# Four dense feed forwards: two compensated products of the rounded fp32 type in place of three of bf16

## The chip, the cores and the metric

The kernel runs on one core of one Trainium2 chip. The metric is the device time of one execution in microseconds. TensorE (PE in the rows), VectorE (DVE), ScalarE (ACT), GpSimd (POOL) and the DMA queues are driven by programs of their own, which wait for each other by semaphores. SyncE (SP) issues the transfers of the weights.

## The reference, cut to what matters

The model is a stack of four layers over 256 tokens of 1024 channels; the first layer also carries 256 context tokens. Each layer has a mixer and a feed forward. The feed forwards touched here are dense and gated:

```python
def swiglu(t, w_gate, w_up, w_down):
    return (silu(t @ w_gate) * (t @ w_up)) @ w_down
x = x + g2 * swiglu(modulate(x, n_ffn, sh2, sc2), wg, wu, wd)
```

All inputs are fp32. There are four such calls: the first layer's on x (hidden width 2816), the same weights on the context (2816), the second layer's (2816) and the third layer's (3584). The fourth layer has eight experts in its place, of which each token uses two; they are computed by other code (`moe_parts`), which stays as it is.

## The kernel before, in words

**Tiling.** A feed forward goes over the hidden width in chunks of 128: 22, 22, 22 and 28 chunks, 94 in all. A chunk's weights are 1.5 MB: the front (gate and up, 128 partitions x 2048 fp32 values, 1 MB) and the back (down, 128 x 1024, 0.5 MB). They come into a ring of four slots in SBUF (`RING`), by the SP queue (`feed`, L334), which issues front c+1 and then back c, each after a wait until the slot's old front or back is released (`front_used`, `back_used`). The plan of the ring goes over the whole program: two blocks of modulation weights stand ahead of each feed forward, one or three behind some of them (`early`, `behind` in the new text; `ada_n`, `behind` in the old).

**Products.** To get near fp32 from bf16, each operand is split in a bf16 head and a bf16 remainder, and each product is made of three: head x head, head x remainder, remainder x head. For a chunk, `up_products` (L971) does the first layer: for gate and up, and for 8 blocks of 128 channels, three products (L984 to L986) with the weights stationary and the 256 tokens moving, so 48 with 256 columns. `down_products` (L989) does the second layer: two token blocks x two halves of the 1024 outputs x three products (L999 to L1001), 12 with 512 columns, the hidden tokens stationary. The outputs stay in four PSUM banks over all chunks.

**Splits.** ScalarE casts the front and the back to bf16 (`cast_hi_loop`, L1190 and L1193; `cast_hi`, L954 and L957, outside the loop). VectorE subtracts (`make_lo`, L964 and L968) and so makes the remainder, writes it to a buffer of its own, and releases the slot at that moment. Heads and remainders have two buffers each, by the chunk's parity. The input of the feed forward is split the same way once (L1091, L1122).

**Order.** PE does first layer c+1, then second layer c, and so on. ScalarE for chunk c: silu (`silu_of`, L1009), cast of front c+2, cast of back c+1. VectorE for chunk c (`gate_of`): product of the silu and the up part (L1016), its cast to bf16 (L1024), its remainder (L1026), then the remainders of front c+2 (L964) and back c+1 (L968). The chunks run in a hardware loop of four per round, with the last two or more outside. At the start of a feed forward the first front is cast and split in halves (L1094, L1095, L1126, L1129), between modulation rows (L494, L502). At its end VectorE multiplies the four banks by the gate row and adds them to x (L1173, L1176), and ScalarE squares (L540).

**The rounded type.** The projections of the mixers (`split_linear`, L767) already split fp32 operands in two parts of the rounded four-byte type (named fp32r where it is written, f32 where products read it) and do three products of it (L830 to L832), with 288 to 512 columns. Their remainders are written over the raw weights in the ring (L875).

The expert code has a second form for many tokens to an expert (`ffn_parts` with `gates`), which is not executed on these inputs; the change keeps it under the name `general_parts`.

Of the kernel before, what the change touches and what calls it, by code (L numbers as in the profile page):

```python
# [19 lines left out]
F32 = mybir.dt.float32  # L20
# [43 lines left out]
FFNS = ("l0_ffn", "l1_ffn", "ffn2", "moe")  # L64

# [42 lines left out]
class Signals:  # L108


    def __init__(self, sig):
# [46 lines left out]
        self.block_made = sig("last_group_block")  # L158

# [57 lines left out]
def build(nc, ctx, d, out):  # L217
# [33 lines left out]
    RINGR = halves_of("weights", SLOTS * SLOT)  # L251
    PS = ctx.enter_context(nc.psum_tensor("ps", [PB, 8, 512], F32))
# [718 lines left out]
    def up_products(pe, j, n, hid, width, h_hi, h_lo, by_half=False):  # L971

        if by_half:
            pe.wait_ge(S.w_lo.sem, S.w_lo.at(1))
        else:
            pe.wait_ge(front_used.sem, n + (place.n + 1))
        pe.wait_ge(S.act_done.sem, n + S.act_done.at(1))
        for w in range(2):
            if by_half and w:
                pe.wait_ge(front_used.sem, place.n + 1)  # L980
# [55 lines left out]
    def ffn_parts(x, f, o, gates=None, gate=GB, first=0, ada_at=None, ada_n=0, behind=0):  # L1036

        a, n = place.n, f // PB * (NE if gates is not None else 1)  # L1040
# [3 lines left out]
        h = HT[:, :, o:o + T]  # L1044
# [4 lines left out]
        def products(pe):  # L1049
# [4 lines left out]
            for i in range(ada_n):  # L1054
                ada_row(pe, i, ada_at)
            zero_products(pe, 2 if ada_n else 14, 5)
            pe.wait_ge(S.h_lo.sem, S.h_lo.at(2))

            def up(j, n, by_half=False):
                up_products(pe, j, n, hid, T, lambda k: h_hi[:, k, :], lambda k: h_lo[:, k, :], by_half)  # L1060
            up(0, 0, gates is None)
            for i in range(ada_n):
                ada_turn(pe, i)
# [8 lines left out]
            for i in range(min(2, behind)):  # L1072
                ada_row(pe, i, a + n, ada_n)
            for i in range(behind):
                ada_turn(pe, i, ada_n)
                if i + 2 < behind:
                    ada_row(pe, i + 2, a + n, ada_n)
            zero_products(pe, max(0, 18 - 8 * behind), 4)

        def squares(act):  # L1080
            for i in range(4):
                if i < behind:
                    ada_row_kept(act, i, ada_n)
                act.wait_ge(S.tail_added.sem, S.tail_added.at(i + 1))
                part_square(act, first + i // 2, i % 2, x[:, i // 2, i % 2 * 512:(i % 2 + 1) * 512])
                if 0 < i <= behind:
                    ada_cols_kept(act, i - 1, a + n, ada_n)

        def silus(act):
            for half in halves:  # L1090
                act.activation(h_hi[:, half, :], h[:, half, :], ACT.Copy).then_inc(S.h_hi.sem, 1)  # L1091
            if gates is None:
                act.wait_ge(front_in[place.n % SLOTS].sem, 16 * (place.n // SLOTS + 1))
                act.activation(gu[0][0][:, 0:D], RING[:, place.n % SLOTS, 0:D], ACT.Copy).then_inc(S.w_hi.sem, 1)  # L1094
                act.activation(gu[0][0][:, D:2 * D], RING[:, place.n % SLOTS, D:2 * D],  # L1095
                               ACT.Copy).then_inc(S.hi_gu.sem, 1)
            for i in range(ada_n):
                ada_row_kept(act, i)
            if gates is None:
                cast_hi(act, 0, 1, 1)  # L1100
                cast_hi(act, 1, 0, 0)
            for i in range(ada_n):
                ada_cols_kept(act, i, ada_at)
# [11 lines left out]
            squares(act)  # L1115

        def gating(dve):
# [6 lines left out]
            if gates is None:  # L1124
# [6 lines left out]
                dve.wait_ge(S.ada_kept.sem, S.ada_kept.at(ada_n))  # L1131
                dve.sem_inc(front_used.sem, 1)
                make_lo(dve, 0, 1, 1)
                make_lo(dve, 1, 0, 0)
            if ada_n:
                ada_bias(dve, ada_n, ada_at)
            if gates is None:
# [1540 lines left out]
```

## Time and profile before

| what | value |
|---|---|
| median of 3 runs | 2676.68 us (2670.01 to 2681.77) |
| span of the profiled execution | 2666.8 us |
| time of that execution beside its span | not given; the median stands 9.9 us above the span |
| busy share of the span: PE / DVE / ACT | 92% / 70% / 55% |
| mean granted TensorE clock | 0.973 |
| HBM read | 671.79 MB, 252 GB/s over the span |

The execution begins with the first layer's mixer; the dense feed forwards of the first layer run from 306 to 665 us, the second layer's from about 1005, the third layer's from about 1365; the experts fill the time from 1770 us on. A product's recorded duration holds its way through the array and overlaps with the next, so the distance from one start to the next tells what a product costs.

### The profile page before, as it was taken

To read this page: it belongs to the slowest core of one execution; us is meant where nothing else is said; L and a number is where in the kernel's file an instruction comes from. 1 tells how busy PE (TensorE), PEld (TensorE's weight loads), DVE (VectorE), ACT (ScalarE), POOL (GpSimd) and SP (SyncE) were. 2 spreads that over 40 slices of the span, in tenths; PEclk is the share of its full clock that TensorE was granted. 3 is DMA by queue.
4 is the path that set the end of the run, shared out by engine and by line. 5 is a ranking of instruction groups with operands and counts; after the bars stand their busy time and mean duration, and the time that the engine had idled before them with its cause. 6 is when DMAs were issued, how large, how long until landed. Compare 5 with 4: busy or idle time off the path is not lost. (4 is left out here: it accounts for less than half of the span.)

```text
span 2666.8 us, 58450 instructions
## 1 busy us (share of the span) xinstructions
PE 2458.1 (92%) x23209; PEld 1851.2 (69%) x23209; DVE 1880.0 (70%) x2489; ACT 1466.4 (55%) x1865; POOL 14.9 (1%) x12
## 2 busy tenths in 40 slices
PE   6988999999898889999899999889999899999997
PEld 4745777677664457768677768667777777777775
DVE  3277555655645566555765555769999999999997
ACT  3146444433421545434454434458888888888885
POOL 0000000000200000000000000000000000000000
PEclk9989999999988999999999999999999999999999
DMA  7340555554456126555375545439999999999995
GB/s 302 116 200 25 223 199 208 214 199 163 150 223 243 75 89 259 207 186 183 140 276 192 210 174 185 163 113 396 411 417 414 417 418 407 419 416 418 418 417 232
DMA packets 121213, 674.38 MB, mean 253 GB/s; under 512 B 13489, under 2 KB 13969, under 8 KB 67089
## 3 DMA queue, kind: packets, MB, share of 16 engines
q1 hardware_dynamic: 120032, 664.47, 64.1%
q10 hardware_dynamic: 1072, 8.42, 0.8%
q8 instruction: 74, 1.21, 0.2%
q14 instruction: 35, 0.28, 0.0%
HBM read 671.79 MB, written 1.05 MB: 252 GB/s over the span
## 5 line engine op out<-in xcount | busy, mean ns | idle before, releaser
L984 PE MATMUL ps<-projected,normed_or_mix 128*128 128x256 bf16 x1504 | 409.9, 273 | 1.5 <-issue 1.5
L985 PE MATMUL ps<-projected,normed_or_mix 128*128 128x256 bf16 x1504 | 409.9, 273 | 0.0
L1383 DVE TENSOR_TENSOR aux<-weights,aux 128x1024 bf16<-128x1024 f32 x223 | 271.2, 1217 | 1.4 <-ACT aux L1329 1.4
L1378 DVE TENSOR_TENSOR turned<-weights,turned 128x2048 bf16<-128x2048 f32 x112 | 256.3, 2288 | 8.9 <-ACT turned L1323 4.2
L1323 ACT ACTIVATE turned<-weights 128x2048 bf16<-128x2048 f32 x112 | 213.6, 1907 | 49.7 <-DMA weights<-moe 47.3
L1329 ACT ACTIVATE aux<-weights 128x1024 bf16<-128x1024 f32 x223 | 232.1, 1041 | 2.1 <-PE ps L1267 1.8
L1254 PE MATMUL ps<-projected,turned 128*128 (+1 forms) x1792 | 232.9, 206 | 0.0
L1253 PE MATMUL ps<-projected,turned 128*128 (+1 forms) x1792 | 232.9, 206 | 0.0
L1255 PE MATMUL ps<-projected,turned 128*128 (+1 forms) x1792 | 232.9, 206 | 0.0
L831 PE MATMUL ps<-weights_halves,normed_or_mix_halves 128*128 128x512 f32 (+4 forms) x576 | 218.6, 380 | 0.0
L1265 PE MATMUL ps<-aux,probs 128*96 128x512 bf16 x448 | 172.6, 385 | 43.4 <-DVE probs L1393 43.4
L986 PE MATMUL ps<-projected,aux 128*128 128x256 bf16 x752 | 205.0, 273 | 0.0
L986 PE MATMUL ps<-projected,normed_or_mix 128*128 128x256 bf16 x752 | 205.0, 273 | 0.0
L1016 DVE TENSOR_TENSOR probs_turned<-probs,ps 128x256 f32<-128x256 f32 x94 | 39.5, 421 | 229.3 <-ACT probs L1009 229.3
L1009 ACT ACTIVATE probs<-ps 128x256 f32<-128x256 f32 x94 | 36.0, 383 | 295.4 <-PE ps L986 295.1
L1254 PEld LDWEIGHTS ps<-projected,turned 128*128 128x128 bf16 x1792 | 175.4, 98 | 6.5
L1253 PEld LDWEIGHTS ps<-projected,turned 128*128 128x128 bf16 x1792 | 175.3, 98 | 5.1
L1255 PEld LDWEIGHTS ps<-projected,turned 128*128 128x128 bf16 x1792 | 175.3, 98 | 0.0
L875 DVE TENSOR_TENSOR weights_halves<-weights,extra_halves 128x948 fp32r<-128x948 f32 (+4 forms) x80 | 92.7, 1165 | 111.9 <-ACT extra_halves L856 111.9
L1267 PE MATMUL ps<-aux,probs 128*96 128x512 bf16 x448 | 169.8, 379 | 0.0
L1266 PE MATMUL ps<-aux,probs 128*96 128x512 bf16 x448 | 169.8, 379 | 0.0
L984 PEld LDWEIGHTS ps<-projected,normed_or_mix 128*128 128x128 bf16 x1504 | 147.5, 98 | 29.4 <-issue 3.4
(399 smaller groups left out, 6365.8 us busy)
## 6 DMA issues: line engine op xcount, KB each, us to landing
weights<-moe SPq DMA_DIRECT2D x224, 1024.0 KB, 8.5
weights<-moe SPq DMA_DIRECT2D x224, 512.0 KB, 6.6
weights<-l_ffn SPq DMA_DIRECT2D x66, 1024.0 KB, 4.9
weights<-ada SPq DMA_DIRECT2D x64, 1024.0 KB, 5.6
weights<-l_ffn SPq DMA_DIRECT2D x66, 512.0 KB, 5.6
weights<-ada SPq DMA_DIRECT2D x64, 512.0 KB, 6.0
weights<-ffn SPq DMA_DIRECT2D x28, 1024.0 KB, 4.9
weights<-w_in SPq DMA_DIRECT2D x24, 948.0 KB, 4.8
```

The costliest lines, as they stand in the source:

```text
L831: pe.matmul(o, h_hi(k)[:, t], lo, start=False, stop=False)
L984: pe.matmul(o, hi, h_hi(k), start=(k == 0), stop=False)
L985: pe.matmul(o, hi, h_lo(k), start=False, stop=False)
L986: mm = pe.matmul(o, lo, h_hi(k), start=False, stop=(k == KD - 1))
L1253: pe.matmul(o, hi[:, t], xh, start=(k == 0), stop=False)
L1254: pe.matmul(o, hi[:, t], xl, start=False, stop=False)
L1255: mm = pe.matmul(o, lo[:, t], xh, start=False, stop=(k == KD - 1))
L1265: pe.matmul(o, hi, w_hi[:, t], start=start, stop=False)
L1323: act.activation(gu4[j % SLOTS][0], RING[:, slot(j), 0:2 * D], ACT.Copy).then_inc(S.hi_gu.sem, 1)
L1329: act.activation(down4[j % SLOTS][0], RING[:, slot(j), 2 * D:3 * D], ACT.Copy).then_inc(S.hi_d.sem, 1)
L1378: dve.tensor_tensor(gu4[j % SLOTS][1], RING[:, slot(j), 0:2 * D], gu4[j % SLOTS][0], ALU.subtract).then_inc(front_used.sem, 1)
L1383: dve.tensor_tensor(down4[j % SLOTS][1], RING[:, slot(j), 2 * D:3 * D], down4[j % SLOTS][0], ALU.subtract).then_inc(back_used.sem, 1)
```

## The change: what it does

In the four dense feed forwards each operand a is split as a lead and a rest of the rounded four-byte type, with L = 128. For a weight w: lead = w / (L + 1), rest = w - L x lead. For an input or hidden value h: lead = L x h, rest = (L + 1) x h - lead. Then w x h is (lead of w) x (lead of h) + (rest of w) x (rest of h) up to what the rounding leaves in second order: two products in place of three.

- `ffn` is written out for itself; the three closures of `ffn_parts` remain for the experts' second form only.
- PE: 2 x 8 x 2 = 32 products for a chunk's first layer, 8 for its second. The rests of the weights are read from the ring itself.
- ScalarE: scaled copies make the leads of the weights, and now also the lead of the hidden product, after the copy of front c+2.
- VectorE: one multiply-add with an immediate makes each rest, and writes a weight's rest over its slot. The rest of the hidden product stands behind the rest of front c+2.
- PE, not VectorE, releases the slots: the front at the end of a first layer, the back at the end of a second.
- The first chunk is still split in halves, and the modulation rows keep their place.

```diff
+LEAD = 128.0
+        h_lead, h_rest = (PR[:, i * 2048:(i + 1) * 2048].rearrange("p (k t) -> p k t", k=KD) for i in range(2))
+        w_lead = [[XNR[:, 0:2 * D], XNR[:, 2 * D:3 * D]], [AUXR[:, 0:2 * D], XNR[:, 3 * D:4 * D]]]
+        f_lead = [PbR[:, p * 512 + T:p * 512 + 2 * T] for p in range(2)]
+        f_rest = [PTR[:, p * 512 + T:p * 512 + 2 * T] for p in range(2)]
...
+        def lead_of(act, to, src):
+            return act.activation(to, src, ACT.Copy, scale=1 / (LEAD + 1))
+
+        def rest_of(dve, to, src, lead):
+            return dve.scalar_tensor_tensor(out=to, in0=lead.bitcast(F32), scalar=-LEAD, in1=src, op0=ALU.mult,
+                                            op1=ALU.add)
+
+        def up(pe, j, c, first=False):
+            if first:
+                pe.wait_ge(S.w_lo.sem, S.w_lo.at(1))
+            else:
+                pe.wait_ge(S.rest_gu.sem, c + S.rest_gu.at(1))
+            pe.wait_ge(S.prod.sem, c + S.prod.at(1))
+            for w in range(2):
+                if first and w:
+                    pe.wait_ge(S.rest_gu.sem, S.rest_gu.at(1))
+                    pe.wait_ge(S.ada_kept.sem, S.ada_kept.at(early))
+                for k in range(KD):
+                    t = w * D + k * PB
+                    out_ = hid[j % 2][:, w * T:(w + 1) * T]
+                    pe.matmul(out_, w_lead[j % 2][0][:, t:t + PB], h_lead[:, k, :], start=(k == 0), stop=False)
+                    mm = pe.matmul(out_, ring(RINGR, j, t, t + PB), h_rest[:, k, :], start=False, stop=(k == KD - 1))
+            mm.then_inc(front_used.sem, 1)
+
+        def down(pe, j, c, last=False):
+            pe.wait_ge(S.rest_d.sem, c + S.rest_d.at(1))
+            pe.wait_ge(S.hid_rest.sem, c + S.hid_rest.at(1))
+            for b in range(2):
+                for hf in range(2):
+                    q, t = slice(b * PB, (b + 1) * PB), hf * 512
+                    pe.matmul(PS[:, 2 * b + hf, :], f_lead[j % 2][:, q], w_lead[j % 2][1][:, t:t + 512], start=False,
+                              stop=False)
+                    mm = pe.matmul(PS[:, 2 * b + hf, :], f_rest[j % 2][:, q],
+                                   ring(RINGR, j, PART + t, PART + t + 512), start=False, stop=last)
...
+            mm.then_inc(back_used.sem, 1)
...
+        def silu_and_lead(act, j, c, gate_up=lambda: None):
+            p = j % 2
+            act.wait_ge(front_used.sem, c + (c0 + 1))
+            act.wait_ge(S.prod.sem, c + S.prod.at(1))
+            act.activation(silu[p], hid[p][:, 0:T], ACT.Silu).then_inc(S.silu_done.sem, 1)
+            gate_up()
+            act.wait_ge(S.prod.sem, c + S.prod.at(3))
+            act.wait_ge(back_used.sem, c + (c0 - 1))
+            act.activation(f_lead[p], f_of[p], ACT.Copy, scale=LEAD).then_inc(S.hid_lead.sem, 1)
...
+        def product_and_rest(dve, j, c, gate_up=lambda: None):
+            p = j % 2
+            dve.wait_ge(S.silu_done.sem, c + S.silu_done.at(1))
+            dve.tensor_tensor(f_of[p], silu[p], hid[p][:, T:2 * T], ALU.mult).then_inc(S.prod.sem, 1)
+            gate_up()
+            dve.wait_ge(S.hid_lead.sem, c + S.hid_lead.at(1))
+            dve.scalar_tensor_tensor(out=f_rest[p], in0=f_of[p], scalar=LEAD + 1, in1=f_lead[p].bitcast(F32),
+                                     op0=ALU.mult, op1=ALU.subtract).then_inc(S.hid_rest.sem, 1)
...
+                with pe.Fori(0, rounds) as g:
+                    for j in range(SLOTS):
+                        up(pe, j + 1, g * SLOTS + (j + 1))
+                        down(pe, j, g * SLOTS + j)
...
+                with act.Fori(0, rounds) as g:
+                    for j in range(SLOTS):
+                        c = g * SLOTS
+                        silu_and_lead(act, j, c + j, lambda: gate_up_lead(act, j + 2, c + (j + 2), g))
+                        down_lead(act, j + 1, c + (j + 1), g)
...
+                with dve.Fori(0, rounds) as g:
+                    for j in range(SLOTS):
+                        c = g * SLOTS
+                        product_and_rest(dve, j, c + j, lambda: gate_up_rest(dve, j + 2, c + (j + 2)))
+                        down_rest(dve, j + 1, c + (j + 1))
```

## Rows read from the trace of the kernel before

**Rows 1.** The page, busy tenths of PE, and GB/s, in 40 slices.
```profile
PE   6988999999898889999899999889999899999997
GB/s 302 116 200 25 223 199 208 214 199 163 150 223 243 75 89 259 207 186 183 140 276 192 210 174 185 163 113 396 411 417 414 417 418 407 419 416 418 418 417 232
```

**Rows 2.** Windows: stretch, its us, busy us of each engine, clock, DMA share, GB/s.
```profile
340.00:475.00 135.00, 135.00 (x1036) 101.21 (x1035) 77.63 (x85) 59.37 (x56) 0.00 (x0) 1.00 0.56 201
```

**Rows 3.** Groups of instructions by line (busy us, mean ns of one, idle before).
```profile
L984 PE MATMUL ps<-projected,normed_or_mix 128*128 128x256 bf16 x1504 | 409.9, 273 | 1.5 <-issue 1.5
L1009 ACT ACT_TABLE_LOAD x16 | 20.5, 1283 | 54.6 <-PE ps L986 54.4
```

**Rows 4.** Timeline of one chunk: start us, duration us, instruction [idle before].
```profile
340.65 0.27 PE L984 MATMUL ps<-projected,normed_or_mix 128*128 128x256 bf16 x1
340.65 0.10 PEld L985 LDWEIGHTS ps<-projected,normed_or_mix 128*128 128x128 bf16 x1
...
345.89 0.38 PE L999 MATMUL ps<-aux,probs 128*128 128x512 bf16 x1
...
348.48 0.27 PE L984 MATMUL ps<-projected,normed_or_mix 128*128 128x256 bf16 x1
```

**Rows 5.** Timeline of the projection's last two groups, 512 and 288 columns.
```profile
754.69 0.39 PE L830 MATMUL ps<-extra_halves,normed_or_mix_halves 128*128 128x512 f32 x1
...
758.09 0.29 PE L830 MATMUL ps<-extra_halves,normed_or_mix_halves 128*128 128x288 f32 x1
758.09 0.19 PEld L831 LDWEIGHTS ps<-weights_halves,normed_or_mix_halves 128*128 128x128 f32 x1
758.22 0.19 PEld L832 LDWEIGHTS ps<-extra_halves,turned_halves 128*128 128x128 f32 x1
...
762.06 0.29 PE L830 MATMUL ps<-extra_halves,normed_or_mix_halves 128*128 128x288 f32 x1
```

**Rows 6.** Timeline of ScalarE and VectorE around a table load.
```profile
340.47 2.29 DVE L964 TENSOR_TENSOR aux<-weights,normed_or_mix 128x2048 bf16<-128x2048 f32 x1 [0.59 <-ACT normed_or_mix L1190]
342.68 1.22 DVE L968 TENSOR_TENSOR normed_or_mix<-weights,normed_or_mix 128x1024 bf16<-128x1024 f32 x1
...
346.15 1.28 ACT L1009 ACT_TABLE_LOAD   x1 [4.18 <-PE ps L986]
347.44 0.38 ACT L1009 ACTIVATE probs<-ps 128x256 f32<-128x256 f32 x1
347.72 1.90 ACT L1190 ACTIVATE normed_or_mix<-weights 128x2048 bf16<-128x2048 f32 x1
...
349.66 2.29 DVE L964 TENSOR_TENSOR normed_or_mix<-weights,normed_or_mix 128x2048 bf16<-128x2048 f32 x1 [0.59 <-ACT normed_or_mix L1190]
```

**Rows 7.** Lines by themselves (ns min/median/max) and groups of multiply-adds (busy us, mean ns).
```profile
L856 ACT ACTIVATE projected_halves<-weights x32: 1042/1057/1128, 244.5 to 1745.0; 128x1024 fp32r<-128x1024 f32 x32
L1193 ACT ACTIVATE aux<-weights x42: 1045/1057/1059, 321.0 to 1549.1; 128x1024 bf16<-128x1024 f32 x42
L2517 DVE SCALAR_TENSOR_TENSOR normed_or_mix<-x_sb,small,row_params 128x1024 f32<-128x1024 f32 x2 | 2.5, 1283 | 0.0
L2065 DVE SCALAR_TENSOR_TENSOR aux<-aux 128x512 f32<-128x512 f32 x2 | 1.4, 684 | 0.0
```

**Rows 8.** DMA issues of the page: KB each, median us from issue to landing.
```profile
weights<-l_ffn SPq DMA_DIRECT2D x66, 1024.0 KB, 4.9
```

**Rows 9.** Timeline at the first feed forward's start and end.
```profile
312.46 2.29 DVE L964 TENSOR_TENSOR aux<-weights,normed_or_mix 128x2048 bf16<-128x2048 f32 x1 [0.76 <-ACT normed_or_mix L954]
...
315.90 1.40 PE L502 MATMUL ps<-square_consts,k_turned 128*128 128x3 f32 x12
...
322.40 0.38 PE L999 MATMUL ps<-normed_or_mix,probs 128*128 128x512 bf16 x1
...
482.44 0.69 DVE L1173 TENSOR_TENSOR extra<-ps,gate_rows 128x512 f32<-128x512 f32 x1 [1.61 <-PE ps L1001]
...
489.11 2.00 ACT L1091 ACTIVATE projected<-turned 128x1024 bf16<-128x1024 f32 x2 [0.46 <-PEq L1200]
```

More of the change, by code:

```diff
@@ L1034, in ffn_done, with general_parts @@
             s.done(n)
-    def ffn_parts(x, f, o, gates=None, gate=GB, first=0, ada_at=None, ada_n=0, behind=0):
-        a, n = place.n, f // PB * (NE if gates is not None else 1)
+    def general_parts(x, f, gates, gate=GB):
+        a, n = place.n, f // PB * NE
         hid = [PS[:, 4 + p, :] for p in range(2)]
@@ L1071, in products @@
                 down_products(pe, c, c, outs, stop=(c == n - 1), each=S.bank_done if c == n - 1 else None)
[L1072 to L1087, printed above, removed]
+            zero_products(pe, 18, 4)
         def silus(act):
@@ L1195, in ffn @@
     def ffn(x, f, o, gate=GB, first=0, behind=0):
-        a, n, beside = place.n, f // PB, 2
-        place.n += beside
-        products, silus, gating = ffn_parts(x, f, o, gate=gate, first=first, ada_at=a, ada_n=beside, behind=behind)
+        a, n, early = place.n, f // PB, 2
+        c0 = a + early
+        hid = [PS[:, 4 + p, :] for p in range(2)]
+        h = HT[:, :, o:o + T]
+        h_lead, h_rest = (PR[:, i * 2048:(i + 1) * 2048].rearrange("p (k t) -> p k t", k=KD) for i in range(2))
@@ L1202, in _ @@
             def _(sp):
-                feed(sp, a + SLOTS, a + beside + n + behind + SLOTS)
+                feed(sp, a + SLOTS, c0 + n + behind + SLOTS)
             @block.tensor
             def _(pe):
-                products(pe)
+                for bank in range(4):
+                    pe.matmul(PS[:, bank, :], Z16[:, 0:PB], Z16[:, :], start=True, stop=False)
+                for i in range(early):
+                    ada_row(pe, i, a)
+                zero_products(pe, 2, 5)
+                pe.wait_ge(S.h_lo.sem, S.h_lo.at(2))
@@ L1213, in _ @@
+                for i in range(4):
+                    if i < behind:
+                        ada_row_kept(act, i, early)
+                    act.wait_ge(S.tail_added.sem, S.tail_added.at(i + 1))
+                    part_square(act, first + i // 2, i % 2, x[:, i // 2, i % 2 * 512:(i % 2 + 1) * 512])
+                    if 0 < i <= behind:
+                        ada_cols_kept(act, i - 1, c0 + n, early)
             @block.vector
             def _(dve):
[L1215 to L1216 removed]
```

206 lines of the change are left out of this document (124 added, 82 removed).

## The prediction

> **What bounds the kernel now.** I read the page first [rows 1]: TensorE is busy in nine tenths or more of most slices until the experts begin, and there the transfers take over, at over 400 GB/s. The change touches only the four dense feed forwards, so the next view is the windows [rows 2]: inside a feed forward PE is busy all the time (135.00 of 135.00 us), VectorE 58% of it, ScalarE 44%, the DMA engines 56%, at a granted clock of 1.00, which is the 2.4 GHz level. So the feed forwards are bound by TensorE and by nothing else. The groups [rows 3] give the counts: L984 has 1504 products, so 94 chunks of 16, and three products for each pair.
>
> The durations in those groups (273 ns) overlap, so I take the time from one start to the next from the timeline [rows 4]. The first layer's products of one chunk run from 340.65 to 345.89: 48 in 5.24 us, 0.109 each. The second layer's run from 345.89 to 348.48: 12 in 2.59 us, 0.216 each. Together 7.83 us, and 94 x 7.83 = 736 us, 28% of the span.
>
> **The change, part by part.**
>
> *First layer's products.* 48 of bf16 with 256 columns become 32 of the rounded type with 256. No row shows that type at 256 columns. The nearest rows are the projections [rows 5]: at 512 columns 15 steps take 3.40 us (0.2267 each), at 288 columns 30 steps take 3.97 us (0.1323 each). Between them a column costs 0.42 ns, and 32 columns below the narrower one give 0.119. The bounds: 0.109, the bf16 pitch at the same width, since four-byte operands showed no gain anywhere; and 0.132, the 288 pitch, which holds whatever part of it is a floor under narrow products. I take 0.119, as it is nearest to the 288 row. So 32 x 0.119 = 3.80 us, 1.44 less. The weight load is the point of doubt: recorded at 0.19 us for four bytes, 0.10 for bf16 [rows 4, 5]. But at 288 columns the next load starts 0.13 us after the last one, while the last one is still on record, so loads overlap each other and the products.
> A rule speaks against this. The Trainium skill, TensorE: Matmul & The Clock Gate, section "The mechanism" (what overlaps and what doesn't), lets a load overlap running products only when it targets another row group; its section "LDWEIGHTS (loading the stationary operand)" gives 128/1.2 = 107 ns. By these an estimate is 32 x (107 + 107) ns + 8 x (107 + 213) ns = 9.4 us a chunk. The trace disagrees for both types: a bf16 load of 0.10 and a product of 107 ns fit in a pitch of 0.109.
>
> *Second layer's products.* 12 become 8 at 512 columns: 8 x 0.2267 = 1.81 us, 0.78 less. A chunk on PE is then 5.61 us, 2.22 less.
>
> *ScalarE.* The two casts become scaled copies into the four-byte type, and the cast of the hidden product moves here from VectorE. The type costs nothing: 1057 ns in L856 and in L1193 for 1024 columns [rows 7]. Busy per chunk: 1.90 + 1.06 + 0.38 (silu) + 0.38 (new; same size as the silu) = 3.7 us, below 5.61.
>
> *VectorE.* Subtractions become a multiply-add with an immediate, written over the slot. Such an operation costs what a subtraction costs (L2065, 512 columns, 684 ns, against 0.69 for one of two tensors), and with two pointers and 1024 columns 1283 ns against 1.22 us [rows 6, 7, 9]. I take 2.29 + 1.22 + 0.42 + 0.43 = 4.4 us; 0.13 more if the pointer form is right. Under 5.61 again. The cast L1024 goes.
>
> *The new chain.* A chunk's second layer needs its hidden remainder, and on VectorE that now stands behind the remainder of the gate and up weights two chunks ahead, which waits for ScalarE. From the moment PE leaves the first layer [rows 4, 6]: 0.26 until ScalarE starts, 0.28 to its next instruction, 1.94 for the lead cast and the handover (347.72 to 349.66), 2.21 to the next VectorE instruction (340.47 to 342.68), 0.43, and 0.06 to PE: 5.18 us. PE has 1.81 + 3.80 = 5.61 us of other products, so this is hidden by 0.4. A table load adds 1.29 (346.15 to 347.44): 6.47, a stall of 0.86. There are 16 [rows 3]: one at the start of each of three feed forwards, and 13 in the loops, one in each later round of four. 13 x 0.86 = 11 us is given back.
> The Trainium skill, ScalarE: Activation LUTs, section "What ACT_TABLE_LOAD costs", adds a drain of 1.38 us to each load. With it the sum would lose 18 us more, an estimate. The silu at 347.44 stands right behind the load, so the trace shows no drain.
>
> *Slots.* A slot's front is now released by PE at the end of its products, not by VectorE, and the SP queue issues in the order front, back, so each issue waits for PE. Front c+4 is issued when the first layer of c ends and is needed by ScalarE two chunks later, 11.2 us on; it lands in 4.9 us (median) [rows 8]. Traffic rises from 201 GB/s to 1.57 MB per 5.61 us = 280 GB/s, against 417 reached in the experts [rows 1, 2]. At the ends, the last slots are freed by PE within its last 9 us instead of before them; but the block behind starts at 489.1, 6.7 us after the first of VectorE's final additions, and first asks for modulation rows, whose slots are freed earlier [rows 9]. I cost all this at nothing; its cover is those margins.
>
> *Start.* [rows 9] In the first feed forward VectorE finishes the second chunk's front at 314.75, unchanged. PE's first chunk now ends near 314.4, the turns of the modulation rows (1.4 us) follow, and the second chunk's first layer ends at 319.6. But the first second layer waits for the chain: table load near 316.1, silu 317.4, lead 317.65 to 319.55, remainder to 321.8, hidden remainder 322.2. Before, it began at 322.40. So the two first chunks' first layers gain nothing, 0.1 us in all; where no table load stands at the start (the context's feed forward) 1.3 more.
>
> *End.* VectorE's eight final operations from 482.44 on, 0.69 each, set the end, started by the first bank; of the last second layer only one bank's share (0.2) is gained, and about 0.15 lost to the hidden chain (1.96 us against 1.81).
>
> **Sum.** With 22 chunks: 20 x 1.44 + 21 x 0.78 + 0.15 = 45.3 us, three times, plus 1.3: 137. With 28: 26 x 1.44 + 27 x 0.78 + 0.15 = 58.6. Together 196, less 11 for the table loads: 185 us. The profile gives no time of its execution beside the span of 2666.8; 2666.8 - 185 = 2481.8, and the median of the runs stands 9.9 above the span, so **2492 us**.
> Bounds by the pitch: at 0.109 (and 0.216) the same sum is 230 - 16 = 213, 2464 us. At 0.132 it is 159 - 6 = 153, 2524 us.
>
> **The rivals.**
> 1. *Each load shows (slower).* If at 256 columns a four-byte load isn't hidden, a first layer's product costs 0.188 + 0.107 = 0.295: 9.4 + 1.8 = 11.2 us a chunk, 3.4 more, 94 times: 2998 us. By the page's rule above, with 9.4 us a chunk, it would be about 2825, an estimate. The point that decides is (7.83 - 1.81) / 32 = 0.188 a product, 42% above the 288 row. For it: the doubled load record and that no row is as narrow. Against it: rows 5. 3%.
> 2. *VectorE paces (no change).* If the multiply-add into the four-byte type took two passes, its 2048 and 1024 columns would take 4.4 and 2.3 us, the hidden one 0.7: 7.8 us a chunk, what it is now, near 2675 us. For it: no row has it that long. Against: 1283 ns at 1024. 3%.
> 3. *The transfers pace.* If holding the slots longer kept the rate at the present 205 GB/s or little above, a chunk would take 1.57 MB / 0.22 TB/s = 7.1 us and save 0.7: 94 x 0.7 = 66 us, 2611. For it: every issue now waits for PE. Against: two chunks of slack. 5%.
> 4. *The chain shows in every chunk.* If handovers add 0.7 us to 5.18, it exceeds 5.61 by 0.27; a held second layer delays the next but one first layer, so half of that shows in each chunk: 94 x 0.14 = 13 us, and 13 x 0.7 = 9 at the table loads: 2514. It has only 0.4 us of cover. 9%, inside the range.
>
> The forecast with its bounds has 80%. **Range** 2462 to 2535: from the lower bound to beyond the upper one, with rival 4 in it; rivals 1 to 3 are left out. About 0.5% (13 us) is what a measurement of this kernel can tell from no change. Faster by more: 0.8 + 0.05 + 0.09 = 0.94; within it 0.03; slower 0.03.
>
> **What would show it.** In the changed profile: 40 products a chunk, 32 of them starting 0.119 apart and 8 at 0.227; table loads 22.4 + 0.9 = 23.3 us apart; after each load a gap on PE of 0.9 us before the second layer, and none elsewhere; VectorE's 2048-column rows at 2.29; ScalarE waiting for PE, never for a landing; granted clock 1.00; the experts unchanged at about 417 GB/s. I am wrong if the pitch at 256 columns is over 0.132, if PE idles before a first layer (released by VectorE's remainder: rival 2; with ScalarE waiting for DMA: rival 3), or if the second layer waits in every chunk (rival 4).

## The result, and the profile after

| | before | after |
|---|---|---|
| median, four runs of each | 2675.76 us (2670.01 to 2681.77) | 2511.55 us (2505.05 to 2511.93) |
| span of the profiled execution | 2666.8 us | 2503.3 us |
| its own time | not given | 2505.05 us |

The ratio of the medians is 0.9381 (0.9361 to 0.9401): faster. The forecast was 2492 us with a range of 2462 to 2535, so it was 20 us too low and the range holds the result.

The page of the changed kernel, 40 slices of the span: busy tenths of PE, granted clock, GB/s (they answer to [rows 1]).

```profile
PE   6988999998977789999999899889999999999997
...
PEclk9979999999988999999999998999999999999999
...
GB/s 306 134 218 1 127 269 255 276 278 198 148 228 267 1 165 258 267 193 182 193 271 269 273 174 133 138 346 417 411 417 415 418 418 408 418 417 418 417 417 214
```

The experts are as they were, at 417 GB/s. In the middle of the feed forwards the transfers rose from about 200 to between 255 and 278 GB/s. The same shows in the windows (stretch, its us, busy us of PE, PEld, DVE, ACT and POOL, granted clock, DMA share, GB/s); the two short ones are the first second layers of the first and the third of the four feed forwards (the first layer's and the second layer's):

```profile
340.00:475.00 135.00, 128.66 (x898) 115.30 (x899) 95.27 (x96) 84.08 (x103) 0.00 (x0) 1.00 0.74 268
326.50:329.70 3.20, 3.12 (x8) 2.49 (x9) 3.20 (x3) 1.01 (x2) 0.00 (x0) 0.51 0.62 246
944.00:948.00 4.00, 3.54 (x10) 2.90 (x11) 4.00 (x5) 1.39 (x2) 0.00 (x0) 0.57 0.57 226
```

In [rows 2] PE was busy for 135.00 of 135.00 us; now 6.3 us of that stretch are not. VectorE went from 58% to 71%, ScalarE from 44% to 62%. PE is still what the chunks go by, but something holds it up now and then. The timeline of PE over one chunk (start us, duration us, instruction):

```profile
341.28 0.28 PE L1180 MATMUL ps<-projected_halves,normed_or_mix_halves 128*128 128x256 f32 x1
341.39 0.28 PE L1181 MATMUL ps<-projected_halves,weights_halves 128*128 128x256 f32 x1
...
345.11 0.40 PE L1190 MATMUL ps<-normed_or_mix_halves,probs_halves 128*128 128x512 f32 x1
...
346.95 0.28 PE L1180 MATMUL ps<-projected_halves,aux_halves 128*128 128x256 f32 x1
```

Read against [rows 4]: 32 products in 3.83 us, 0.1197 each, then 8 in 1.84 us, 0.230 each. A chunk is 5.67 us where it was 7.83. What holds PE up is on the timeline of all engines around a table load (in brackets the idle time before an instruction and what ended it), the counterpart of [rows 6]:

```profile
345.37 1.28 ACT L1216 ACT_TABLE_LOAD   x1 [2.30 <-PE ps L1181]
346.67 0.38 ACT L1216 ACTIVATE probs<-ps 128x256 f32<-128x256 f32 x1
346.95 1.90 ACT L1161 ACTIVATE normed_or_mix_halves<-weights 128x2048 fp32r<-128x2048 f32 x1
348.75 0.41 ACT L1220 ACTIVATE probs_halves<-probs_turned 128x256 fp32r<-128x256 f32 x1
...
348.88 2.29 DVE L1164 SCALAR_TENSOR_TENSOR weights_halves<-normed_or_mix_halves,weights 128x2048 fp32r<-128x2048 f32 x1 [1.38 <-ACT normed_or_mix_halves L1161]
351.10 0.42 DVE L1237 SCALAR_TENSOR_TENSOR probs_turned_halves<-probs_turned,probs_halves 128x256 fp32r<-128x256 f32 x1
351.66 0.47 PE L1190 MATMUL ps<-normed_or_mix_halves,probs_halves 128*128 128x512 f32 x1 [0.71 <-DVE probs_turned_halves L1237]
...
369.02 1.28 ACT L1216 ACT_TABLE_LOAD   x1 [2.30 <-PE ps L1181]
```

PE leaves the first layer at 345.11. The load, the silu, the lead of the gate and up weights two chunks ahead, its rest, and then the rest of the hidden product stand in line, and PE gets that last one 6.55 us later. The next load stands 23.65 us behind this one; four chunks are 4 x 5.67 = 22.68, so each load costs 0.97 us: 0.88 before the second layer (6.55 - 5.67), and about 0.08 more because its first product after a wait takes 0.30 us to the next one, not 0.23.

At the start of the first feed forward the same chain shows at its full length, and the products behind it are slow:

```profile
320.29 1.28 ACT L1216 ACT_TABLE_LOAD   x1
...
321.86 1.91 ACT L1161 ACTIVATE normed_or_mix_halves<-weights 128x2048 fp32r<-128x2048 f32 x1
...
326.01 0.42 DVE L1237 SCALAR_TENSOR_TENSOR probs_turned_halves<-probs_turned,probs_halves 128x256 fp32r<-128x256 f32 x1
326.58 0.77 PE L1190 MATMUL ps<-normed_or_mix_halves,probs_halves 128*128 128x512 f32 x1 [2.64 <-DVE probs_turned_halves L1237]
327.14 0.63 PE L1192 MATMUL ps<-weights_halves,probs_turned_halves 128*128 128x512 f32 x1
...
329.92 0.28 PE L1180 MATMUL ps<-projected_halves,normed_or_mix_halves 128*128 128x256 f32 x1
```

PE idles 2.64 us, and then its second-layer products start 0.43 us apart instead of 0.23: the granted clock in that window is 0.51, the lower of its two levels (1.2 GHz). This second layer takes 3.34 us instead of 1.84; of the difference 1.4 us are the clock's, since one that begins after a wait at the full clock takes 1.92 (the third layer's in this profile). The waits by what they were for (us in total, times, longest) say who is late and who isn't:

```profile
ACT probs L1216 <- PE ps L1181: 156.6, 74, 2.7
...
DVE weights_halves L1164 <- ACT normed_or_mix_halves L1161: 66.3, 49, 1.5
...
DVE weights_halves L1164 <- ACT aux_halves L1161: 42.9, 43, 1.4
...
ACT L1216 <- PE ps L1181: 29.9, 13, 2.3
```

ScalarE waits for PE, VectorE for ScalarE; in no row does ScalarE wait for a transfer inside the feed forwards.

**Where the time went, by stage.** From the timeline I took each feed forward from ScalarE's first copy of its input to the end of the mean-square chain behind it, and what lies between them, in us of one profile each:

| | FF 1 | context | FF 2 | FF 3 | the four | span less the four |
|---|---|---|---|---|---|---|
| before | 183.13 | 185.59 | 187.81 | 234.78 | 791.31 | 1875.5 |
| after | 144.86 | 140.20 | 148.93 | 182.51 | 616.50 | 1886.8 |

The four feed forwards, which are all that the change touches, gave 174.8 us. The rest, whose code is the same, took 11.3 us more in this profile: 4.1 in the stretch from 136 us to the first feed forward, 1.8 between the context's and the second layer's, 0.4 between the second and the third layer's, 5.1 in the mixer behind the third layer's, nothing in the experts. The next section looks at whether that is the change's.

### The profile page after: what moved, and what is told of

Same layout as the page of the kernel before. It is cut to its first block and busy times, and to the rows that moved or that the text cites. A ratio compares the mean times of both kernels' runs of the same rounds, so it can differ in the third digit from the quotient of the medians.

```text
span 2503.3 us, 54795 instructions
## 1 busy us (share of the span) xinstructions
PE 2268.8 (91%) x21306; PEld 1811.3 (72%) x21329; DVE 1844.2 (74%) x2395; ACT 1490.5 (60%) x1959; POOL 14.9 (1%) x12
## 3 DMA queue, kind: packets, MB, share of 16 engines
HBM read 671.79 MB, written 1.05 MB: 269 GB/s over the span
## 5 line engine op out<-in xcount | busy, mean ns | idle before, releaser
L1181 PE MATMUL ps<-projected_halves,weights_halves 128*128 128x256 f32 x1504 | 364.9, 284 | 0.0
L1181 PEld LDWEIGHTS ps<-projected_halves,weights_halves 128*128 128x128 f32 x1504 | 288.6, 192 | 3.4
L1164 DVE SCALAR_TENSOR_TENSOR weights_halves<-normed_or_mix_halves,weights 128x1024 fp32r<-128x1024 f32 (+1 forms) x145 | 222.6, 1537 | 66.3 <-ACT normed_or_mix_halves L1161 66.3
L1161 ACT ACTIVATE normed_or_mix_halves<-weights 128x1024 fp32r<-128x1024 f32 (+1 forms) x145 | 188.8, 1304 | 10.9 <-PE ps L1192 10.9
L1180 PE MATMUL ps<-projected_halves,normed_or_mix_halves 128*128 128x256 f32 x752 | 182.5, 284 | 1.5 <-issue 1.5
L1180 PE MATMUL ps<-projected_halves,aux_halves 128*128 128x256 f32 x752 | 182.5, 284 | 0.0
L1190 PE MATMUL ps<-normed_or_mix_halves,probs_halves 128*128 128x512 f32 x376 | 151.0, 402 | 18.9 <-DVE probs_turned_halves L1237 18.5
```

The source lines that it names most:

```text
L1161: return act.activation(to, src, ACT.Copy, scale=1 / (LEAD + 1))
L1164: return dve.scalar_tensor_tensor(out=to, in0=lead.bitcast(F32), scalar=-LEAD, in1=src, op0=ALU.mult, op1=ALU.add)
L1180: pe.matmul(out_, w_lead[j % 2][0][:, t:t + PB], h_lead[:, k, :], start=(k == 0), stop=False)
L1181: mm = pe.matmul(out_, ring(RINGR, j, t, t + PB), h_rest[:, k, :], start=False, stop=(k == KD - 1))
```

## Experiments

### The two kernels again

Edit: none in either.

> The kernel before once more, nothing edited, to see what its stages repeat. Theory (the stages that the change doesn't touch move by some us with the granted clock, in either kernel): the stretch from the first rotary step to the first feed forward and the one of the last scan mixer differ by 2 to 6 us from the first profile, the four feed forwards stay at 183.1, 185.6, 187.8 and 234.8 within 1 us. Rival (the stages repeat to a tenth of a us, and the changed kernel's 11 us more are its own): every stretch as in the first profile.

> The changed kernel once more, nothing edited, to see what repeats. Theory (all that the change does lies in the four feed forwards, the rest of the difference is the TensorE clock in stages it doesn't touch): the four feed forwards take 144.9, 140.2, 148.9 and 182.5 us again within 2 us each, a round of four chunks 23.65 us, while the stages before the first feed forward and between them move by some us either way, with the granted clock. Rival (the change lengthens the other stages by 11 us, by its place in the program or by what it leaves behind): those stages show the same +4.0, +1.8, +0.5 and +5.1 us as in the first profile. Ratio to before 0.938 in both.

**Measured.** The kernel before: 2673.4 us in one run, the feed forwards 183.13, 185.59, 187.80 and 234.78, the same to 0.01 us. The changed kernel: 2507.23 us against 2679.3 beside it, ratio 0.9361 (0.9332 to 0.9389); its feed forwards took 144.97, 140.19, 148.91 and 183.93, in sum 618.00. The third layer's is 1.4 us longer than in the first profile, and in this one the granted clock fell at its start too.

**What follows.** The feed forwards repeat, so an effect can be read from their sum to within 1.5 us, which is what one fall of the clock makes. The rest doesn't: in the two profiles of the kernel before, the stretch from 136 us to the first feed forward is 170.1 and 172.5 us long, the last mixer 164.7 and 168.9. In the changed one they are 174.3 and 170.4, and 169.8 and 164.7, and there the granted clock goes with it: from 136 to 180 us it was 0.57 in the longer and 0.77 in the shorter. The experts move too: 901.9 and 902.0 us before, 901.8 in the first profile of the changed kernel and 910.4 in the second, with nothing edited between these two. So single stages of the same code differ by 2 to 9 us from profile to profile.

Whether the sum of these stages is longer for the changed kernel is less clear. The span less the feed forwards is 1875.5 and 1880.3 us for the kernel before, and 1886.8 and 1887.2 for the changed one. For the two-product kernel below, whose code is the old one but for the products left out, it is 1886.8 as well, so the new code is not needed for it. The median less the feed forwards is:

| runs beside each other | before | changed kernel and its variants |
|---|---|---|
| the first (four each) | 1884.5 | 1895.1 |
| changed kernel again and the next three below | 1888.0 | 1889.2, 1890.1, 1890.0, 1888.6 |
| narrower products, PE busy (one run each) | 1881.6, 1882.1 | 1893.1, 1893.3 |
| both starts mended | 1890.0 | 1891.3 |

Twice it is 1 to 2 us more, and twice about 11. So the 11 us are not shown to be the change's, nor shown not to be: that stays open.

### One silu ahead of the loop

```diff
                 down_lead(act, 0, 0)
+                act.activation(SM[:, 250:251], SM[:, 250:251], ACT.Silu)
                 for i in range(early):
```

> ScalarE does one silu of one column ahead of the modulation copies, before the loop of each feed forward, so that the table is already loaded when the loop begins. Theory (the 13 loads inside the loops each hold the second layer by 0.96 us, and the three at the start sit in the chain to the first second layer): table loads in the feed forwards fall from 16 to 3, one before each of the three loops, a round takes 22.7 us instead of 23.65, the idle of PE before the first second layer falls from 2.6 to 1.3 us as in the context's feed forward, and the time falls by 13 x 0.96 + 3 x 1.3 + 3 for the clock behind the idle, about 19 us: ratio to before 0.931. Rival (the loads are hidden and the gap has another cause, the remainders on VectorE): rounds stay at 23.65 and the time within 3 us of the changed kernel. Second rival: the load is placed in the loop again, 16 remain, nothing changes.

**Measured.** 2487.72 us, ratio 0.9296 (0.9270 to 0.9323); the feed forwards 597.62 us, 20.4 less than the changed kernel run beside it. The table loads of L1216 are gone from all rounds, and three are left, at the new line (the line by itself, and the timeline at the start of the first feed forward, with PE's first second layer in it and in the second and third layers'):

```profile
L1283 ACT ACT_TABLE_LOAD  x3: 1283/1283/1283, 315.9 to 1242.6; - x3
```

```profile
315.92 1.28 ACT L1283 ACT_TABLE_LOAD   x1
317.22 0.20 ACT L1283 ACTIVATE small<-small 128x1 f32<-128x1 f32 x1
...
318.80 0.39 ACT L1216 ACTIVATE probs<-ps 128x256 f32<-128x256 f32 x1
...
323.98 0.47 PE L1190 MATMUL ps<-normed_or_mix_halves,probs_halves 128*128 128x512 f32 x1 [1.55 <-DVE probs_turned_halves L1237]
...
935.65 0.47 PE L1190 MATMUL ps<-normed_or_mix_halves,probs_halves 128*128 128x512 f32 x1 [1.35 <-DVE probs_turned_halves L1237]
...
1250.41 0.47 PE L1190 MATMUL ps<-normed_or_mix_halves,probs_halves 128*128 128x512 f32 x1 [1.35 <-DVE probs_turned_halves L1237]
```

**What follows.** This is a one-column instruction that computes nothing that is used. It makes the silu's table the one that stands when the loop is entered, and then the program loads none inside. In the changed kernel, as in the one before, a load stood in every round of three feed forwards, though silus and plain copies are all that ScalarE does there. The load now lies in idle time of ScalarE. The sum fits: 13 stalls of 0.97 are 12.6 us; in three starts the wait falls from 2.6 us to 1.55, 1.35 and 1.35, together 3.6; and the clock stays up after the shorter wait, three times 1.4 us: 20.4.

### The hidden product's split ahead of the weights'

```diff
             act.activation(silu[p], hid[p][:, 0:T], ACT.Silu).then_inc(S.silu_done.sem, 1)
-            gate_up()
...
             act.activation(f_lead[p], f_of[p], ACT.Copy, scale=LEAD).then_inc(S.hid_lead.sem, 1)
+            gate_up()
```

The same on VectorE: the rest of the hidden product stands ahead of the rest of the gate and up weights.

> The hidden product's lead and rest go ahead of the next front's lead and rest, on ScalarE and on VectorE. Theory (the order in the change hides the handover between the two engines; with the hidden values first, each turn of VectorE holds product 0.45, ScalarE's lead of the hidden 0.30, its copy of the front 1.94, the front's rest 2.21 and the back's rest 1.15, 6.05 us in a ring, over PE's 5.67): a chunk takes 6.05 us, table loads no longer show at PE, about 0.38 x 90 - 13 = 21 us more than the changed kernel, ratio to before 0.946. Rival (the chain to the second layer is what costs, and shortening it pays): no gap behind table loads, a round at 22.7 us, 12 us less than the changed kernel, ratio 0.934.

**Measured.** 2518.05 us, ratio 0.9403 (0.9374 to 0.9432); the feed forwards 628.09 us, 10.1 more than the changed kernel. A wait at the first layer takes the place of the one at the second (timeline of ScalarE and PE):

```profile
346.28 0.40 PE L1190 MATMUL ps<-normed_or_mix_halves,probs_halves 128*128 128x512 f32 x1
...
348.46 0.39 PE L1180 MATMUL ps<-projected_halves,normed_or_mix_halves 128*128 128x256 f32 x1 [0.18 <-DVE weights_halves L1164]
...
349.90 0.42 ACT L1219 ACTIVATE probs_halves<-probs_turned 128x256 fp32r<-128x256 f32 x1 [2.61 <-DVE probs_turned L1234]
...
352.38 0.40 PE L1190 MATMUL ps<-normed_or_mix_halves,probs_halves 128*128 128x512 f32 x1
...
358.44 0.40 PE L1190 MATMUL ps<-normed_or_mix_halves,probs_halves 128*128 128x512 f32 x1
```

A chunk is 358.44 - 352.38 = 6.06 us, where 5.67 of PE's are products.

**What follows.** In this order the two engines make a ring: lead of the weights on ScalarE, rest of the weights and of the back on VectorE, the next hidden product behind them, its lead on ScalarE, and only then the next lead of weights. Its length of 6.06 us is in every chunk, so the order that the change chose is the better one in the steady state; the chain that it leaves has 0.4 us of room except at a table load. The ring's length was foreseen to 0.01 us, the effect on the time only by half (21 expected, 10.1 measured in the feed forwards). The expectation left out the starts: the waits before the four first second layers (9.2 us in the second profile of the changed kernel) and the slow clock behind three of them (4.3) are gone here, and in three starts a wait of 1.4 us before the third chunk's first layer takes their place. That makes about 11.6 of the 21; the rest isn't told apart.

### Two bf16 products in place of three

The kernel before with two of its three products in the dense feed forwards; its casts, its remainders and its order stay. It leaves out a product that near-fp32 results need, so it only serves to tell the count of the products from their type.

```diff
                 pe.matmul(o, hi, h_hi(k), start=(k == 0), stop=False)
-                pe.matmul(o, hi, h_lo(k), start=False, stop=False)
                 mm = pe.matmul(o, lo, h_hi(k), start=False, stop=(k == KD - 1))
...
                 pe.matmul(PS[:, bank, :], hi[:, o], w_hi[:, c], start=start, stop=False)
-                pe.matmul(PS[:, bank, :], hi[:, o], w_lo[:, c], start=False, stop=False)
-                mm = pe.matmul(PS[:, bank, :], lo[:, o], w_hi[:, c], start=False, stop=stop)
+                mm = pe.matmul(PS[:, bank, :], hi[:, o], w_lo[:, c], start=False, stop=stop)
```

> The kernel before with two of its three bf16 products for each pair, in the dense feed forwards (in the first layer the product of the head with the input's remainder is left out, in the second that of the hidden remainder with the head); everything else, also the splits, stays. It tells the count of the products from their type. Theory (a chunk is what PE issues): 32 x 0.109 + 8 x 0.216 = 5.22 us a chunk, no gap at table loads, since there the hidden remainder stands ahead of the front's on VectorE; about 225 us less than before, ratio 0.916. Rival (at this pace VectorE is the limit: 2.29 + 1.22 + 0.42 + 0.29 + 0.43 and the waits between, about 5.4 to 6 us in a ring with ScalarE): PE waits for VectorE's remainders in every chunk, 5.5 to 6.0 us a chunk, ratio 0.925 to 0.94.

**Measured.** 2439.41 us, ratio 0.9119 (0.9088 to 0.9150); the feed forwards 550.80 us, 240.5 less than before. The timeline of ScalarE over one round of four chunks:

```profile
344.36 0.38 ACT L1007 ACTIVATE probs<-ps 128x256 f32<-128x256 f32 x1 [0.73 <-PE ps L985]
349.58 0.38 ACT L1007 ACTIVATE probs<-ps 128x256 f32<-128x256 f32 x1 [2.09 <-PE ps L985]
...
360.08 1.28 ACT L1007 ACT_TABLE_LOAD   x1 [2.16 <-PE ps L985]
...
365.24 0.38 ACT L1007 ACTIVATE probs<-ps 128x256 f32<-128x256 f32 x1 [0.73 <-PE ps L985]
```

A chunk is 5.22 us, and so is a quarter of the round with the load in it (20.88 / 4).

**What follows.** With as many products as the changed kernel, the old chain hides the table load in the loop. The likely reason is that there the hidden product's cast and remainder stand on VectorE right behind the product; the run before, in which that order hides the loads in the changed kernel too, fits this. At three starts PE does wait, 0.91 us before the third chunk's first layer. The rounded type and the new chain are what parts the two kernels, 618.0 - 550.8 = 67.2 us, and it divides into 94 x 0.45 = 42.3 for the products of the rounded type, 13 x 0.97 = 12.6 for the loads in the loops, 9.2 for the waits at the four starts and 4.3 for the clock behind three of them, less 3 x 1.08 = 3.2 by which the bf16 kernel's own third chunk is late: 65.2. The last 2 us are not told apart.

### Narrower products

```diff
-                for k in range(KD):
-                    t = w * D + k * PB
-                    out_ = hid[j % 2][:, w * T:(w + 1) * T]
+                for q, k in itertools.product(range(2), range(KD)):
+                    t, z = w * D + k * PB, slice(q * PB, (q + 1) * PB)
+                    out_ = hid[j % 2][:, w * T + q * PB:w * T + (q + 1) * PB]
```

Both products then read the columns `z` only: 64 of 128 columns for 32 of 256.

> Each first-layer product of the changed kernel is cut in two of 128 columns: 64 a chunk in place of 32, with the same values. It shows what of the 0.120 us is streamed columns and what is weight load. Theory A (a product costs its columns at 2.4 GHz and about 13 ns, loads are hidden even at 128 columns): 64 x 0.066 = 4.2 us for the first layer, 0.4 more a chunk, about 35 us more than the changed kernel. Theory B (a four-byte load has a floor of its own between 0.066 and 0.120): the starts lie at that floor; at 0.107, 64 x 0.107 = 6.8 us, 3.0 more a chunk, 280 us more, slower than before. In either case the second layer's 8 products stay at 0.23.

**Measured.** 2827.22 us in one run, against 2672.85 beside it: slower than the kernel before. The feed forwards took 934.17 us. The timeline of PE in a first layer:

```profile
345.81 0.27 PE L1180 MATMUL ps<-projected_halves,aux_halves 128*128 128x128 f32 x1
345.93 0.27 PE L1181 MATMUL ps<-projected_halves,weights_halves 128*128 128x128 f32 x1
...
352.62 0.28 PE L1181 MATMUL ps<-projected_halves,weights_halves 128*128 128x128 f32 x1
```

and, from the kernel before, the experts' bf16 products of 96 columns:

```profile
1902.66 0.21 PE L1253 MATMUL ps<-projected,normed_or_mix 128*128 128x96 bf16 x1
1902.70 0.21 PE L1254 MATMUL ps<-projected,normed_or_mix 128*128 128x96 bf16 x1
1902.75 0.21 PE L1255 MATMUL ps<-projected,normed_or_mix 128*128 128x96 bf16 x1
```

Two more rows bear on it: from the changed kernel, the four-byte products of the modulation rows, with new weights each and 3 columns; and from the narrow run, products at the lower clock (0.50 from 326 to 333 us):

```profile
318.60 1.40 PE L508 MATMUL ps<-square_consts,k_turned 128*128 128x3 f32 x12
```

```profile
326.64 0.41 PE L1180 MATMUL ps<-projected_halves,aux_halves 128*128 128x128 f32 x1
326.85 0.41 PE L1181 MATMUL ps<-projected_halves,weights_halves 128*128 128x128 f32 x1
```

**What follows.** From the first to the last of the narrow products are 61 steps in 6.81 us, 0.1116 each, hardly less than the 0.1197 of twice the columns; the granted clock there is 1.00. The line through the wider products (0.1197 at 256, 0.230 at 512) would give 0.065. It is a floor that doesn't go by the columns: from the second to the last of the twelve products with 3 columns the starts lie 0.112 us apart as well. At the lower clock it is 0.213 us. Bf16 products, also with new weights each, start every 0.043 us. The loads of the twelve start 0.11 to 0.12 us apart in the trace. The second product starts only 0.03 us after the first, which a product of 256 columns had held back, and each one from the second on starts 0.03 us after its load does. So it is the loads that go at this pace, and the narrow products follow them. That speaks for the load as what sets the floor; no run has such products without a load, which would show it. If it is so, rival 1 named the right mechanism and a wrong size: the floor lies 0.008 us below the pitch at 256 columns. The change as it is stands just clear of it, and cutting the tokens in two loses more than the change gains.

### PE busy while it waits

```diff
                     ada_turn(pe, i)
-                with pe.Fori(0, rounds) as g:
+                up(pe, 1, 1)
+                pe.wait_ge(S.ada_out.sem, S.ada_out.at(early))
+                zero_products(pe, 12, 6)
+                down(pe, 0, 0)
...
+                with pe.Fori(1, rounds) as g:
```

Twelve products of zeros stand ahead of the first second layer, and the first round is written out.

> Behind the second chunk's first layer PE does 12 products of zeros (2.6 us) in each feed forward, where the changed kernel's PE stood idle for 2.6 us before the first second layer, and the first round is written out ahead of the loop. In the changed kernel's profile the granted clock fell to 0.5 behind that idle in the first and third of the four feed forwards, not in the fourth. Theory (the idle brings the fall): no fall, the first second layer takes 1.84 us in all four, 1.5 us less twice; and with the first round outside the loop one table load less in the loop of three feed forwards, about 3 us less. Rival (the fall comes from something else): the clock is at 0.5 again in two of them.

**Measured.** 2507.86 us in one run; the feed forwards 143.38, 141.24, 147.49 and 182.46 us. The window at the first second layer:

```profile
323.00:327.00 4.00, 3.96 (x23) 3.04 (x22) 4.00 (x5) 2.76 (x3) 0.00 (x0) 1.00 0.58 237
```

**What follows.** The granted clock is 1.00 at all four starts, and the three feed forwards in which it had fallen are 1.6, 1.4 and 1.5 us shorter than in the second profile of the changed kernel. That is about what the first second layer gains there: 3.31 to 3.40 us with the clock down, 1.90 to 1.92 here. The context's, in which nothing had fallen, is 1.05 us longer, which is what the filling and the written-out round cost. The chain still sets the start. That one table load fewer was expected is a miss: with the first round written out on PE alone there are still 16.

### Both starts mended

The silu ahead of the loop, and the hidden product's split first in chunk 0 alone, so that a delay of the weights behind it can come only once in a feed forward; the first round is written out on ScalarE and VectorE.

```diff
+                act.activation(SM[:, 250:251], SM[:, 250:251], ACT.Silu)
...
+                for c in range(SLOTS):
+                    silu_and_lead(act, c, c, lambda: gate_up_lead(act, c + 2, c + 2), ahead=(c == 0))
+                    down_lead(act, c + 1, c + 1)
+                with act.Fori(1, rounds) as g:
```

> The silu ahead of the loop, as in the run before, and in the first chunk alone the hidden product's lead and rest ahead of the third front's; the first round is written out ahead of the loop. In the run with the silu ahead PE idles 1.55 us before the first second layer, which waits for the third front's rest, 2.2 us of VectorE that it doesn't need. Theory: the first second layer starts straight behind the second chunk's first layer, and the third front's rest, 0.8 us later than now (near the end of the first second layer), holds PE by 0.3 us at most; so 1.2 us less in each feed forward, their sum 597.6 - 5 = 593 us, and the time 5 us below that kernel's, ratio to before 0.928; the medians alone can't tell 5 us, the stage sums can. Rival: the delay of the third front's rest shows whole, as in the run with the hidden values first in every chunk: the sum stays at 597 to 598.

**Measured.** 2483.90 us against 2681.31, ratio 0.9276 (0.9250 to 0.9302); the feed forwards 592.58 us, 5.0 less than with the silu alone. The timeline at the first start:

```profile
317.14 0.42 ACT L1221 ACTIVATE probs_halves<-probs_turned 128x256 fp32r<-128x256 f32 x1 [0.49 <-DVE probs_turned L1237]
...
317.59 0.42 DVE L1241 SCALAR_TENSOR_TENSOR probs_turned_halves<-probs_turned,probs_halves 128x256 fp32r<-128x256 f32 x1 [0.48 <-ACT probs_halves L1221]
...
319.93 0.40 PE L1190 MATMUL ps<-normed_or_mix_halves,probs_halves 128*128 128x512 f32 x1
```

**What follows.** The operands are there 1.9 us before PE comes to them, and the wait is gone. The delayed weights cost little: the distance from this second layer to the next is 5.90 us, 0.2 over the 5.67. Of what the changed kernel gave back, 618.0 - 592.6 = 25.4 us are won again; this is the fastest version that computes all of it. Against the silu alone the medians differ by less than their intervals, so that last step rests on the stage sums.

## Why the prediction was right, and where it was off

- **The bound.** Right. TensorE set the time of the dense feed forwards before and does after; fewer products made them 22% shorter.
- **First layer.** 0.119 us a product from the line between two widths; 0.1197 measured. It was the term with the most weight, and it was reached by extrapolation over 32 columns. Nothing in the prediction shows that the line holds there, and the floor of 0.112 lies just underneath; that it held to 256 columns was in part luck. A row of the kernel before could have told: the twelve four-byte products of L502 [rows 9], with 3 columns, start 0.112 us apart. The lower bound of 0.109 was below that floor.
- **Second layer.** 0.2267 forecast, 0.230 measured. With the first layer's 0.03 us this makes a chunk 5.67 us, not 5.61: over the 86 first and 90 second layers that the sum counts, 5.3 us.
- **The rule on loads.** By the Trainium skill, TensorE: Matmul & The Clock Gate, sections "The mechanism" and "LDWEIGHTS (loading the stationary operand)", a chunk would have been 9.4 us, an estimate. It is 5.67, so the loads overlap the products, and the passage on row groups doesn't describe this kernel; the same section "The mechanism" also has loads pulled ahead into a background weight buffer, which the pitch agrees with. The measured floor of 0.112 us does lie near the 107 ns for a load that the prediction took from the Trainium skill, but for four-byte operands alone.
- **ScalarE, VectorE.** Right: 1.90, 1.05, 0.38 and 0.41 us, and 2.29, 1.22, 0.42 and 0.42. The multiply-add into the rounded type costs what the subtraction did. Rival 2 is out.
- **The chain.** 5.18 + 1.29 = 6.47 us forecast, 6.55 measured; a stall of 0.86 forecast, 0.97 measured, 13 times, 1.4 us in all. It doesn't show in the other chunks, so rival 4 is out. The run with the silu ahead of the loop shows that the loads are the cause: without them every stall goes.
- **The drain.** The Trainium skill, ScalarE: Activation LUTs, section "What ACT_TABLE_LOAD costs", has 1.38 us more at each load. The silu begins 1.30 us after its load, which lasts 1.28: no drain here.
- **Transfers and slots.** Right at nothing: 268 GB/s, 4.8 us from issue to landing, no wait for a landing. Rival 3 is out.
- **Start.** The time of the first second layer was nearly right: forecast 16.2 us behind the first copy of the input, measured 16.57 (16.42 before), so each start is 0.14 us worse than the nothing that the sum took, 0.6 us over the four. What the prediction lacked is that a wait of 2.6 us on PE costs more than its length. The second layer behind it ran at the lower clock in two feed forwards of the first profile and in three of the second, 1.4 us each time.
- **The sum.** 184.7 us forecast for the feed forwards, 174.8 measured, 9.9 short: 5.3 for the chunk, 1.4 for the stalls, 2.8 for the clock, 0.6 for the starts, which is 0.2 more than there is to explain. The other 11.3 us between the spans of 2481.8 and 2503.3 came from stages whose code the change doesn't touch. No term of the prediction stood for that, though the three times of before lay 12 us apart. Repeated profiles show single stages moving by 2 to 9 us with nothing edited; whether the sum of them is longer by the change is open. So of the 20 us by which the forecast was low, about half is terms of the sum that were sized too small or left out, and about half has no known cause.

## What to carry to other kernels

Cost a product by the distance from start to start at the nearest widths, and look for a row with few columns to see where the floor lies. When an engine gets faster, follow the longest chain that its next operand goes through, handover by handover: here it had 0.4 us of room, and everything that exceeded it showed in full. A function that is alone with its table in a loop should be used once ahead of the loop, where ScalarE idles.

## What the runs showed of the hardware that was not expected

- A row of four-byte products with new weights each starts every 0.112 us, with 128 columns as with 3, and every 0.213 us (128 columns) at the lower clock; bf16 products with new weights and 96 columns start every 0.043 us.
- After 2.6 us without work on PE the granted clock was at its lower level during the second layer that followed (3.3 us) in some feed forwards and not in others: in the first and second layers' in both profiles of the changed kernel, in the third layer's in one of two after the same wait. After the waits of 1.3 to 1.55 us (six in the two profiles and in the run with the silu ahead) it never fell.
- A table load stands in each round of a loop when the table at its entry is another one, though the loop needs only one: 16 loads in three feed forwards, 3 once the silu's table stands at the entry. In the context's feed forward, which follows directly on the first, there is none; that it finds the silu's table standing is the likely reason.
- The same code takes up to 5 us more or less in a stage of some 170 us from one profile to the next, and up to 9 us in the experts' 902. From 136 to 180 us, where PE is sparsely used, the granted clock was 0.57 in the profile with the longest stage (174.3 us) and 0.77 in those of 170.1 and 170.4. The feed forwards of the kernel before, in which PE is busy all the time (135.00 of 135.00 us from 340 us on), repeat within 0.01 us.
